# Gram products of the delta rule as three fp32r products of high and low parts on 64-row halves, with another table of side steps

## The reference, cut to what matters

```python
qc = chunks(l2_norm(q)) * (dk ** -0.5)
kc = chunks(l2_norm(k))
...
lower = jnp.where(strict, jnp.einsum("bhnid,bhnjd->bhnij", k_beta, kc) * decay, 0.0)
...
qk = jnp.where(tri, jnp.einsum("bhnid,bhnjd->bhnij", qc, kc) * decay, 0.0)
```

## Time and profile before

| | us |
|---|---|
| median of 3 runs | 780.93 (780.56 to 781.03) |
| the profiled execution's own time | 781.4 |
| its span, first to last instruction | 779.7 |
| PE busy in it | 771.3 (99%) |
| POOL, ACT, DVE busy | 394.1, 353.5, 324.4 |

### The profile page before, as it was taken

How to read it: one execution, slowest core, us unless ns; L and a number is a source line. 1 busy time by engine, 2 the same in 40 slices (tenths; PEclk the granted TensorE clock), 3 DMA queues, 4 the chain that set the end, 5 groups by cost and what they waited for, 6 DMA issues and landing times.

```text
span 779.7 us, 12435 instructions
## 1 busy us (share of the span) xinstructions
PE 771.3 (99%) x4355; PEld 636.1 (82%) x4355; DVE 324.4 (42%) x499; ACT 353.5 (45%) x631; POOL 394.1 (51%) x347
## 2 busy tenths in 40 slices
PE   8999999999999999999999999999999999999996
PEld 8788788888887878888888888888888888888885
DVE  4596989871463555555506301111013212122225
ACT  6746852268455446445426633332334333333333
POOL 4446984534355344574446454445444444444444
PEclk9999999999999999999999999999999999999999
DMA  7236233323212121223821233233332323322222
GB/s 223 69 94 204 67 82 85 103 70 83 69 43 79 43 69 52 86 79 97 285 94 55 81 109 94 82 106 98 101 93 85 108 96 98 102 95 94 94 81 108
DMA packets 60314, 75.18 MB, mean 96 GB/s; under 512 B 6088, under 2 KB 45552, under 8 KB 60272
## 3 DMA queue, kind: packets, MB, share of 16 engines
q1 hardware_dynamic: 59920, 74.34, 31.5%
q10 hardware_dynamic: 352, 0.28, 0.1%
HBM read 72.49 MB, written 2.11 MB: 96 GB/s over the span
## 4 chain that ended last, share of the span: by engine, by line
PE 96%; DVE 1%; DMA 1%; POOL 0%; ACT 0%; issue 0%; SPq 0%; ACTq 0%; DVEq 0%; POOLq 0%
PE bank L527 29%; PE bank L528 28%; PE bank L529 28%; PE bank L757 1%; PE bank L780 1%; PE bank L767 1%; PE bank L670 1%; DVE y_out L1285 1%; PE bank L721 1%; PE bank L661 1%; DVE tmp L1539 1%; DMA x_sb<-in_x 1%; PE bank L685 1%; PE bank L732 1%; PE bank L852 0%; PE bank L545 0%
## 5 line engine op out<-in xcount | busy, mean ns | idle before, releaser
L1627 POOL TENSOR_TENSOR w_lo<-raw,w_hi 128x512 fp32r<-128x512 f32 x245 | 317.5, 1302 | 359.8 <-ACT w_hi L976 358.5
L976 ACT ACTIVATE w_hi<-raw 128x512 fp32r<-128x512 f32 (+1 forms) x246 | 154.1, 630 | 259.6 <-PE bank L529 254.5
L527 PE MATMUL bank<-h_hi,w_hi 128*128 128x512 f32 (+1 forms) x558 | 217.6, 390 | 0.1
L528 PE MATMUL bank<-h_lo,w_hi 128*128 128x512 f32 (+1 forms) x558 | 212.8, 381 | 0.0
L529 PE MATMUL bank<-h_hi,w_lo 128*128 128x512 f32 (+1 forms) x558 | 212.7, 381 | 0.0
L527 PEld LDWEIGHTS bank<-h_hi,w_hi 128*128 128x128 f32 x558 | 105.1, 188 | 24.7 <-issue 4.8
L529 PEld LDWEIGHTS bank<-h_hi,w_lo 128*128 128x128 f32 x558 | 105.1, 188 | 20.6
L528 PEld LDWEIGHTS bank<-h_lo,w_hi 128*128 128x128 f32 x558 | 105.3, 189 | 18.5
L527 PE MATMUL bank<-w_hi,a_hi 128*128 128x512 f32 x256 | 99.7, 389 | 0.1
L529 PE MATMUL bank<-w_hi,a_lo 128*128 128x512 f32 x256 | 99.6, 389 | 0.0
L528 PE MATMUL bank<-w_lo,a_hi 128*128 128x512 f32 x256 | 99.6, 389 | 0.0
(11 more groups left out here) (266 smaller groups left out, 879.4 us busy)
## 6 DMA issues: line engine op xcount, KB each, us to landing
raw<-in_w_in SPq DMA_DIRECT2D x87, 256.0 KB, 2.8
raw<-in_w_mlp_out SPq DMA_DIRECT2D x64, 256.0 KB, 2.6
raw<-in_w_mlp_in SPq DMA_DIRECT2D x62, 256.0 KB, 2.6
raw<-in_w_out SPq DMA_DIRECT2D x16, 256.0 KB, 2.7
decay<-row_copy SPq DMA_DIRECT2D x4, 512.0 KB, 5.2
raw<-in_w_branch_att SPq DMA_DIRECT2D x8, 256.0 KB, 2.8
raw<-in_w_branch_dn SPq DMA_DIRECT2D x8, 256.0 KB, 2.7
x_res<-in_x SPq DMA_DIRECT2D x1, 2048.0 KB, 8.6
```

The lines of the kernel that those rows point to most:

```text
L527: pe.matmul(o, s_hi, m_hi, start=start, stop=False, skip_group_check=True)
L528: pe.matmul(o, s_hi, m_lo, start=False, stop=False, skip_group_check=True)
L976: return a.activation(o, i_, ACT.Copy, scale=scale)
L1627: g.tensor_tensor(w_lo[:, slot, :], raw[:, slot, :], w_hi[:, slot, :].bitcast(F32), ALU.subtract).then_inc(lo_ready, 1)
```

## The change

`gr` no longer multiplies `qk_dn` in fp32. Eight new ACT steps `sh` copy each query and key tile to `qk_hi` (fp32r), eight new POOL steps `sl` subtract it to give `qk_lo`, and PE makes each product in three passes. For each pair of heads the two heads lie on rows 0 to 63 and 64 to 127, and their matmuls alternate. `qk_hi` lies where `qk_att` is written later, `qk_lo` in two free places. The table of side steps is another one.

```diff
-    "bt": (5,),
-    "b1": (12,),
-    "b2": (12,),
+    "bt": (4,),
+    "b1": (10,),
+    "b2": (11,),
...
-    "cv": (4, 7, 7, 9, 12, 16, 16, 16, 20, 22, 24, 26),
-    "sg": (5, 7, 9, 10, 12, 16, 17, 19, 21, 25, 25, 29),
-    "gk": (19, 20, 20, 21),
-    "dec": (20, 21, 23, 23),
-    "ta": (19, 20, 24, 26),
-    "gr": (21, 23, 25, 27),
-    "ld": (21, 25, 27, 28),
-    "rt": (21, 24, 25, 27),
-    "sc": (28,),
+    "cv": (4, 7, 8, 9, 11, 16, 16, 16, 17, 22, 24, 26),
+    "sg": (4, 7, 9, 10, 12, 17, 17, 19, 20, 25, 25, 29),
+    "sh": (6, 8, 9, 10, 15, 17, 18, 19),
+    "sl": (7, 8, 13, 14, 16, 17, 19, 20),
+    "gk": (19, 21, 21, 24),
+    "dec": (21, 21, 24, 26),
+    "ta": (19, 20, 25, 26),
+    "gr": (22, 23, 24, 26),
+    "ld": (22, 27, 27, 28),
+    "rt": (22, 24, 25, 27),
+    "sc": (27,),
...
-    "ma": (49, 49),
-    "mb": (50, 50),
+    "ma": (49, 51),
+    "mb": (51, 54),
...
-    "py": (55, 65, 77, 83),
-    "pb": (56, 67, 78, 84),
-    "sb": (57, 70, 79, 86),
-    "sa": (61, 71, 80),
+    "py": (55, 66, 73, 79),
+    "pb": (56, 67, 75, 81),
+    "sb": (57, 70, 76, 83),
+    "sa": (60, 71, 77),
...
+    qk_hi = at("qk_hi", 178, [P, 2, 4, S], F32R)
+    qk_lo = at("qk_lo", 56, [P, 2, 24, S], F32R)
...
             elif name == "gr":
-                pe.wait_ge(silu_done, 8)
+                pe.wait_ge(qklo_ready, 8)
                 for q in (0, 2):
                     two = [open_fill(f + q), open_fill(f + q + 1)]
                     for j in range(2):
-                        for hh in range(2):
-                            r = slice(hh * HD, hh * HD + HD)
-                            x_ = pe.matmul(two[hh][:, j * 256:j * 256 + 256], qk_dn[r, 4 + q + j, tok],
-                                           qk_dn[r, q + j::4, tok], start=True, stop=True)
-                            if j == 1:
-                                x_.then_inc(side_full, 1)
+                        for p_, (k_, m_) in enumerate(((qk_hi, qk_hi), (qk_hi, qk_lo), (qk_lo, qk_hi))):
+                            for hh in range(2):
+                                r = slice(hh * HD, hh * HD + HD)
+                                x_ = pe.matmul(two[hh][:, j * 256:j * 256 + 256], k_[r, 1, q + j, tok], m_[r, 0:2, q + j, tok],
+                                               start=p_ == 0, stop=p_ == 2, skip_group_check=True)
+                                if j == 1 and p_ == 2:
+                                    x_.then_inc(side_full, 1)
...
+            elif name == "sh":
+                mark(copy(qk_hi[:, i // 4, i % 4, :], qk_dn[:, i, :]), qkhi_ready)
...
-            if name == "gk":
+            if name == "sl":
+                g.wait_ge(qkhi_ready, i + 1)
+                mark(g.tensor_tensor(qk_lo[:, i // 4, i % 4, :], qk_dn[:, i, :], qk_hi[:, i // 4, i % 4, :].bitcast(F32),
+                                     ALU.subtract), qklo_ready)
+            elif name == "gk":
```

More of the change, by code:

```diff
@@ L347, in program @@
     silu_v_done = sem("silu_v_done")
+    qkhi_ready = sem("qkhi_ready")
+    qklo_ready = sem("qklo_ready")
     ba_args = sem("ba_args")
```

## The result

The changed kernel takes 786.11 us (median of 4 runs, 785.45 to 788.29), the kernel before 780.84 beside it: a ratio of 1.0069, 95% interval 1.0057 to 1.0081. It is 5.3 us slower where 1.9 were forecast, and 786.11 lies above the range. Timed again later (run `a2_changed_kernel_again`, 5 runs) it took 785.48 against 780.91, ratio 1.0054 [1.0040, 1.0067], 4.6 us. The profiled execution is the slowest of its runs, 788.29, with a span of 786.3 where before had 779.7.

A forecast was written before the change was run, and what follows sets the result against it. PE's single queue of matmuls was taken to bound the kernel, each new wait paid in full. The terms -1.2 + 0.85 + 2.0 + 0.24 = +1.9 gave 782.8 us, range 780.8 to 785.5.

The forecast's parts named there:

- The Gram products, -1.2: `gr` on PE: 12 fp32r pairs of 0.12 us save 0.3 us per block, 1.2 us in all.
- The path of PE's other steps, +0.24: Moved side steps on PE: the new table's changes of matmul shape cost 0.24 us more.
- Wait 1, +0.85: Unit 4: `bt` directly behind `ba` waits for ACT's copy to release the bank, +0.85 us.
- Wait 2, +2.0: Unit 26: the fourth `gr`, behind `ta` of block 3, waits for ACT's three passes to release banks, +2.0 us.
- Each such wait is paid in full, as there is no slack behind it: Premise for PE: any new wait in its queue lengthens the run by its whole length.
- Neither is on PE's path … so the splits cost nothing: Units 6 to 20: new `sh` on ACT and `sl` on POOL hide behind the weight splits' lead, 0 us.
- Other places … I cost them at nothing: Other steps that came closer (`py`, `sb`, `ot`, `ap`) each keep 0.5 us or more, so cost 0.
- GpSimd comes late: Rival, chance 0.12: POOL delivers `gk` 3 late, delaying PE's `gr`; +1.5 us more, 784.3 us.
- No pairing: Rival, chance 0.11: fp32r row halves in `gr` don't run side by side; +6.8 in sum, 787.7 us.
- Neither wait: Rival, chance 0.08: banks are released before PE reaches them, so neither wait is paid; 780.0 us.
- ScalarE comes in time: Rival, chance 0.19: ACT finishes `dec` 3 before `ta` 3 starts, unit 26 wait 0.8; 781.6 us.

The follow-up runs named there:

- e1: The changed kernel with `bt` back at unit 5 and the fourth `gr` at unit 27; 786.68 us, ratio 1.0065.
- e3: The changed kernel's new table with the old fp32 Gram products, `sh` and `sl` left out; 785.34 us, ratio 1.0049.
- i1: The kernel before with one wasted root on POOL ahead of the scales, making them late; 784.25 us, ratio 1.0042.
- g1: e1 with the `sl` subtractions of tiles 6 and 7 moved from GpSimd to VectorE; 785.61 us, ratio 1.0061.
- g2: g1 with GpSimd's second and third mask (`gk` 1 and 2) back at unit 20 instead of 21; 784.13 us, ratio 1.0038.
- e2: The changed kernel with pieces of the block inverse (`bi`) moved behind VectorE's evacuations; 787.19 us, ratio 1.0084.
- e7: The changed kernel with row halves not alternating, three products of one half before three of the other; 785.75 us, one execution.
- e4: The kernel before's table with the new products, rows for `sh` and `sl` added; 786.52 us, ratio 1.0062.

## Why the prediction was wrong, and where it was right

- **The Gram products, -1.2**: right. 0.31 per block against the 0.3 taken, with pairs after 0.12. They pair, though no row had shown it. But the gain isn't in the end time.
- **The path of PE's other steps, +0.24**: the attention stage added 0.03 from unit 42 to unit 91. In e1, where neither wait stands in between, units 20 to 29 lose 0.1 beyond the products' gain. Too high, and small.
- **Wait 1, +0.85**: unit 7 stands at +0.82. Right as a mechanism; e1 shows that taking it out gains nothing while VectorE is late, and in e3 it is part of the loss.
- **Wait 2, +2.0**: 2.03 in the list of waits and 2.2 from start to start, for the reasons given, with `gk` 3 ready at 99.1 where 98.7 was reckoned. Right in the same limited sense. What failed here is the premise at the start, "Each such wait is paid in full, as there is no slack behind it": in e1 the two were taken out and gave nothing back.
- **"Neither is on PE's path … so the splits cost nothing"**: here it failed. The cover that I named was the lead of the weight splits, and that held: no unit waited for `w_lo` in after, with 0.9 left at unit 31 (I had 1). But POOL's queue has a second customer: the scales, which gate the inverse on VectorE, whose evacuations release PE's banks at units 36 and 40. I reckoned POOL's queue up to `gk` 3 and stopped. Three units further on, `sc` was 3.1 us late: up to there POOL had 7.2 us more to do than before and 4.1 of idle time to take it from. The profile's shares (DVE 42%, POOL 51%) hid that both are nearly full here: from 112 us to its evacuations at unit 40, VectorE had 2.3 us of idle time to give and 0.4 of slack. In i1 a start 3.0 later and 2.7 of longer instructions, less these two, give 3.0: what is beyond them is paid 1 to 1.
- **"Other places … I cost them at nothing"**: I queued those where a step of the table came closer to the one it waits for. The masks of unit 21 came closer to nothing; they were put behind a wait, ACT's high part, that has nothing to do with them (3.4 us in e3, 3.1 in g1, 1.0 in after, where the splits fill the rest). In g2, with them in front of it again, the scales came 2.3 earlier.
- **A size that no step had**: two-input instructions of VectorE grow by about 1 us when they meet a weight split, 4 times before and 8 times after. In a2 that is 3.8 us beside the 3.0 of the late start.
- **The clock**: no step of the prediction priced a wait at more than its length. In after a wait of 1.9 was followed by 1.6 us more, in a2 the forecast one of 2.1 by 1.5. Which of the two terms left out shows depends on this: in a2 the clock took 1.5 ahead of unit 36 and VectorE 0.9 at unit 40; in after, with no fall there, VectorE took 2.9.
- **The rivals**: *GpSimd comes late* was nearest in mechanism, 784.3, with a price of 1.5 for the wrong customer: it had `gk` 3 late and PE's `gr` behind it. That reading was 0.4 us off; the effect came in elsewhere. *No pairing*, at 787.7, lies nearer to 786.11 by its number, but `gr` took 1.62 and not 2.9. *Neither wait* fell, and so did *ScalarE comes in time*.

What stays open: why g2 and after have 8 long instructions where i1 has 6; the pile of splits behind the scales is the likely cause (e3, without `qk_lo` and with scales as late as in after, has 5, but there PE, which sets the pace of the splits, is later too); no run changed it alone. Why the clock falls behind one wait of 2 us and not behind another stays open too. No kernel tried here beats the one before; by the account one would need POOL to be done with the scales 3 us sooner than in after, without a pile of splits, and the two forecast waits out as well.

## What to carry to other kernels

Follow each engine that gets new work to the last of its customers, not to the first that is tight: add up its queue until it is idle again, and ask at each step on the way who waits for it and for whom that one works. When a step is moved in an in-order queue, list which waits now stand in front of it. And before a gain is summed with waits that lie ahead of another limit, check that limit: where a second engine's chain sets a later point, gains and losses ahead of it are the same nothing. Where two limits lie close together, an experiment that removes one of them shows little; it takes the list of waits of each run to see which one it met.

## What the runs showed of the hardware that was not expected

- The granted clock fell to 0.54 to 0.83 in stretches of 3 us behind waits of PE of 1.9 to 2.8 us in some executions (after and g2 at 147 us; a2, e2, e3 and e7 at 104 to 110; e4 at 94 to 100) and not in others (after at 104 us behind 2.03; e2 in front of `ma` behind 2.0; e1, g1 and i1 behind 1.8 to 1.9). Where it came it cost about 1.6 us in after, a2 and g2, and 1.0 in e4: matmuls of 512 columns stand 0.43 apart, not 0.23. Behind waits of 1.3 and less from unit 4 on it was not seen.
- Fp32r matmuls on 64 rows with 256 columns run both row halves at once, a pair each 0.12 us (after), the time of one full-height matmul of 256 columns, and 24 weight loads of 128 columns fit into the 1.4 us. Writing three of one half ahead of three of the other made no difference (e7, one execution).
- A VectorE instruction with two inputs in SBUF that takes 0.19 us alone (before, at 117.04) took 1.04 beside a GpSimd subtraction of 128x512 (after, at 121.36), and ended 0.05 behind it.
